# A two-block transformer layer on one core: eight modulation tiles contracted on PE, and the normed input's product on DVE

## The chip, the core and the metric

The kernel runs on one core of one Trainium2 chip. The metric is the device time of one execution in microseconds. The engines are PE (matmuls), DVE, ACT, POOL and SP; SP, ACT and POOL also issue DMAs.

## What is computed

Two blocks follow each other on x (1 x 256 tokens x 1024 features). The part that matters here is the beginning of the first:

```
mod = silu(c) @ w_ada + b_ada                    # c: 1 x 1024, w_ada: 1024 x 6144
shift1, scale1, gate1, shift2, scale2, gate2 = split(mod, 6)
h = rms_norm(x, norm1_w) * (1.0 + scale1) + shift1
proj = h @ w_in                                  # q, k, v, conv, index queries, keys and weights
...
x = x + gate1 * (y_mix @ w_out)                  # attention over 64 selected keys, and a short convolution
h2 = rms_norm(x, norm2_w) * (1.0 + scale2) + shift2
x = x + gate2 * peer_ffn(h2, ...)                # 16 of 16384 experts for each of 8 heads and token
x = second_block(x, ...)                         # 2 layers: window attention, gated spatial mixing
```

All of it is in float32.

## The kernel before

The kernel is written engine by engine: each has its own program with waits on semaphores, and nothing is reordered. The order within an engine is the order of its lines.

The input is held transposed, as 8 chunks of 128 features by 256 tokens (`xT`, `hT`). A projection's weights come in units of up to 1 MB (8 chunks by 256 columns) into a ring of four (`wring`, L256). Each 128 columns of a unit are a piece. To reach float32 accuracy with the fast matmul, a piece is split in two rounded parts: ACT makes the high part (`whi`, `split_hi`, L544) and DVE or POOL the low part (`wlo`, `split_lo`, L551); `LO_1` says who. The input is split in the same way (`xh` on ACT at L839, `xl` on DVE in `h_low`, L1575). PE multiplies three of the four combinations (L1155 to L1157). Units 0 and 1 hold the index queries (pieces 0 to 3), unit 2 the index keys and weights (piece 4 and 8 columns more).

The modulation is 48 tiles of 128 columns of w_ada. A tile is loaded transposed, 128 columns on the partitions by 1024 rows, 512 KB, into a ring of five (`ada`). DVE multiplies it by silu(c), which is broadcast over the partitions (`cbc`), and sums along the row (`ada_dots`, L1529). Tiles 0 to 15 give scale1 and shift1, two for each chunk of the input, and come first. SP loads them (`load_ada`, L663), each waiting for the dot that frees its slot, with unit 0 behind the twelfth (`UNIT_0_AFTER`) and units 1 to 3 behind the sixteenth. Later tiles follow certain units (`ADA_AFTER`).

The first stage is then:

- ACT: silu of `cbc`, the squares of x (L818), x times norm1_w into `hT` (L821), the square root (L824). Then for each chunk, once its scale and shift are there, two products with bias (L839), one rounded (`xh`) and one not (`hT`). Pieces 0 and 1 are rounded ahead of chunk 6, pieces 2 and 3 after chunk 7.
- PE: the sum of the squares (L1204), and then the projections (`whole`).
- DVE: for each chunk two dots, the gain (L1585) and the shift with its bias (L1587); the reciprocal of the root after chunk 2's dots (L1583); the lowered chunks as they come. Pieces 0 to 3 are lowered behind chunk 6 and at the end. Then tiles 16 to 23 (`ada_tiles`), whose bias add is L1534, and the index scores (L1604, L1607).
- POOL: `hT` times the reciprocal (L753), then its own pieces from piece 4 on. Piece 12 and later stand behind the mask of the index scores (L759).

SP's queue stands in order too. Unit 6 waits until PE is done with unit 2, since it takes its slot; tiles 21 to 24 are behind units 6 and 7.

After the projections come attention, the experts' stage (two thirds of the span, its pairs of rows gathered by POOL's DMAs) and the second block. None of these is touched.

Of the kernel before, what the change touches and what calls it, by code (L numbers as in the profile page):

```python
# [14 lines left out]
ALU = mybir.AluOpType  # L15
ACT = mybir.ActivationFunctionType
# [6 lines left out]
P = 128  # L23
T = 256
NT = T // P
D = 1024
KC = D // P
# [13 lines left out]
PRING = 4  # L41
WUNIT = KC * 256
WPIECE = KC * P
ADA_RING = 5
UNIT_0_AFTER = 12
ADA_TILES = 6 * D // P
SLOTS, LOW_SLOTS = 14, 8
PAIRS = SLOTS - LOW_SLOTS
# [1 line left out]
EXPERTS = 4  # L50


N1W, N2W, B_ADA, CONV_W, CONV_B, ATT_W, CNV_W, Q_W, K_W, COLS = 0, 8, 16, 64, 76, 80, 84, 88, 89, 90

BQ, BK, BV, BUG, BZG, BZA, LCOLS = 0, 4, 5, 6, 10, 14, 18

# [61 lines left out]

ADA_AFTER = {3: range(16, 21), 6: (21, 22), 7: (23, 24), 8: (25, 26), 9: (27, 28), 18: range(29, 40), }
PIECES_1, SPAN_1 = pieces(UNITS_1[:MIX_UNITS])
LO_1 = "d" * 4 + "p" * 17 + "d" * 16
assert len(LO_1) == len(PIECES_1)
def ada_column(n):

    return n if n >= 2 * KC else n // 2 + (KC if n % 2 == 0 else 0)


def starts(units):  # L130
# [115 lines left out]
def build(nc, a, out):  # L246
    ctx = ExitStack()
    with ctx:
        def sb(name, shape, dt=F32):
            return ctx.enter_context(nc.sbuf_tensor(name, shape, dt))  # L250

        def sem(name):
            return ctx.enter_context(nc.semaphore(name))
# [8 lines left out]
        xT = sb("xT", [P, KC, T])  # L262
        hT = sb("hT", [P, KC, T])
# [58 lines left out]
        u = w1.take(HC * (T + 2)).rearrange("p (c t) -> p c t", t=T + 2)  # L322
        cb = w1.take(HC * T).rearrange("p (c t) -> p c t", t=T)
        yaT = iqT
        relu = p_buf

        w2 = Area(work[:, :])
# [74 lines left out]
        w_loaded = [sem(f"w_loaded{s}") for s in range(RING)]  # L402
        ada_loaded = [sem(f"ada_loaded{s}") for s in range(ADA_RING)]
        ada_used = sem("ada_used")
        last_ada_loaded, last_ada_used = sem("last_ada_loaded"), sem("last_ada_used")
        pool_chain, dve_chain, act_chain = sem("pool_chain"), sem("dve_chain"), sem("act_chain")
        const_ready = sem("const_ready")
        c_silu = sem("c_silu")
        squares = sem("squares")
        sums = sem("sums")  # L410
        h_weighted, rstd_ready, mod_ready = sem("h_weighted"), sem("rstd_ready"), sem("mod_ready")
        std_ready = sem("std_ready")
        h_ready = sem("h_ready")
        h_scaled = sem("h_scaled")
# [242 lines left out]
        def _(sp):  # L657
            sp.dma_start(xT[:, :, :], a["xT"].rearrange("c p t -> p c t")).then_inc(x_loaded, 16)

            def load_ada(n):  # L660
                if n >= ADA_RING:
                    sp.wait_ge(ada_used, n - ADA_RING + 1)
                sp.dma_start(ada[:, n % ADA_RING, :], a["w_ada"][ada_column(n)]).then_inc(ada_loaded[n % ADA_RING], 16)  # L663

            def load_unit(n):
                sp.dma_start(wring[:, n % RING, 0:AT_1[n + 1] - AT_1[n]], a["w1"][:, AT_1[n]:AT_1[n + 1]]).then_inc(w_loaded[n % RING], 16)

            for n in range(2 * KC):
                load_ada(n)
                if n == UNIT_0_AFTER - 1:  # L670
                    load_unit(0)
            for n, (name, at, width, chunks) in enumerate(UNITS_1):
                if n >= RING:
                    was = n - RING
                    if was < MIX_UNITS:
                        split_wait(sp, last_piece(was, PIECES_1))
                        if UNITS_1[was][0] == "idx":
                            sp.wait_ge(proj, DONE_1[last_piece(was, PIECES_1)] + 1)
                    elif UNITS_1[was][0] == "wq":
                        sp.wait_ge(queries, UNITS_1[was][1] // P + 2)  # L680
                    else:
                        sp.wait_ge(expert_scores, UNITS_1[was][1] // (2 * KEYS) + 2)
                if n:
                    load_unit(n)
                for k in ADA_AFTER.get(n, ()):
                    load_ada(k)
                if n == MIX_UNITS + 2:
                    sp.wait_ge(proj, M1)
                    sp.dma_start(last_ada, a["w_ada"][LAST_ADA:].rearrange("n p d -> p n d")).then_inc(last_ada_loaded, 16)
# [42 lines left out]
        def _(pool):  # L732
# [14 lines left out]
            pool.iota(count16[:, :], pattern=[[1, PICKS]], base=0, channel_multiplier=0).then_inc(const_ready, 1)  # L747
            pool.memset(u[:, :, 0:2], 0.0).then_inc(const_ready, 1)

            pool.wait_ge(rstd_ready, 1)  # L750
            for c in range(KC):
                pool.wait_ge(h_weighted, c + 1)
                pool.tensor_tensor(hT[:, c, :], hT[:, c, :], rstd[:, :], ALU.mult).then_inc(h_scaled, 1)  # L753
            for n in range(4, 12):
                split_lo(pool, "p", n)

# [51 lines left out]
        def _(act):  # L808
# [2 lines left out]
            act.dma_start(cols[:, :], a["cols"]).then_inc(cols_loaded, 16)  # L811
            act.wait_ge(c_loaded, 16)
            nc.scalar.activation(cbc, cbc, ACT.Silu).then_inc(c_silu, 1)


            act.wait_ge(x_loaded, 16)
            for c in range(KC):
                nc.scalar.activation(sq[:, c, :], xT[:, c, :], ACT.Square).then_inc(squares, 1)  # L818
            act.wait_ge(cols_loaded, 16)
            for c in range(KC):  # L820
                nc.scalar.activation(hT[:, c, :], xT[:, c, :], ACT.Copy, scale=cols[:, N1W + c:N1W + c + 1]).then_inc(h_weighted, 1)  # L821
            act.wait_ge(const_ready, 2)
            act.wait_ge(sums, 1)
            nc.scalar.activation(rstd[:, :], aux[:, 0, 0:T], ACT.Sqrt, bias=eps[:, 0:1], scale=1.0 / D).then_inc(std_ready, 1)  # L824
            rounded = [0]
# [1 line left out]
            def round_to(n):  # L827

                for k in range(rounded[0], n):
                    split_hi(act, k)  # L830
                rounded[0] = n

            for c in range(KC):
                if 2 * c == UNIT_0_AFTER:
                    round_to(2)
                act.wait_ge(h_scaled, c + 1)
                act.wait_ge(mod_ready, 2 * c + 2)
                for h in (xh, hT):
                    ins = nc.scalar.activation(h[:, c, :], hT[:, c, :], ACT.Identity, bias=mod[:, c:c + 1], scale=gain[:, c:c + 1])  # L839
                ins.then_inc(h_ready, 1)  # L840
            round_to(PRING)

            act.dma_start(wsT[:, :, :], a["wsT"].rearrange("g s t -> s g t")).then_inc(par_loaded, 16)
            act.dma_start(sink[:, :, :].rearrange("p l h -> p (l h)"),
# [294 lines left out]
        def _(pe):  # L1139
# [19 lines left out]
            def input_parts(ready, count):  # L1159

                seen = set()

                def chunk_parts(k):
                    if k not in seen:
                        pe.wait_ge(ready, count(k))
                        seen.add(k)
                    return xh[:, k, :], xl[:, k, :]
                return chunk_parts
# [33 lines left out]
            for c in range(KC):  # L1202
                pe.wait_ge(squares, c + 1)
                ins = mm(aux[:, 0, 0:T], ones[:, :], sq[:, c, :], start=(c == 0), stop=(c == KC - 1))  # L1204
            ins.then_inc(sums, 1)
            h_in = input_parts(h_split, lambda k: k + 1)
            whole(h_in, 3)

# [311 lines left out]
        def _(dve):  # L1520
# [2 lines left out]

            def ada_dots(lo, hi):

                for n in range(lo, hi):
                    dve.wait_ge(ada_loaded[n % ADA_RING], 16 * (n // ADA_RING + 1))
                    tile = ada[:, n % ADA_RING, :]
                    v.tensor_tensor_reduce(tile, tile, cbc, 1.0, 0.0, ALU.mult, ALU.add,  # L1529
                                           mod[:, ada_column(n):ada_column(n) + 1]).then_inc(ada_used, 1)  # L1530

            def ada_bias(lo, hi):
                dve.wait_ge(ada_used, hi)
                chain.link(v.tensor_tensor(mod[:, lo:hi], mod[:, lo:hi], cols[:, B_ADA + lo:B_ADA + hi], ALU.add))  # L1534

            def ada_tiles(lo, hi):
# [30 lines left out]
            def low_to(n):  # L1567

                for k in range(lowered[0], n):
                    split_lo(dve, "d", k)  # L1570
                lowered[0] = n

            def h_low(c):
                dve.wait_ge(h_ready, c + 1)
                v.tensor_tensor(xl[:, c, :], hT[:, c, :], full(xh[:, c, :]), ALU.subtract).then_inc(h_split, 1)  # L1575

            dve.wait_ge(const_ready, 3)

            for c in range(KC):
                ada_dots(2 * c, 2 * c + 2)  # L1580
                if c == 2:
                    dve.wait_ge(std_ready, 1)
                    v.reciprocal(rstd[:, :], rstd[:, :]).then_inc(rstd_ready, 1)  # L1583
                dve.wait_ge(ada_used, 2 * c + 2)
                v.tensor_scalar(gain[:, c:c + 1], mod[:, KC + c:KC + c + 1], cols[:, B_ADA + KC + c:B_ADA + KC + c + 1], ones[:, 0:1],  # L1585
                                ALU.add, ALU.add).then_inc(mod_ready, 1)
                v.tensor_tensor(mod[:, c:c + 1], mod[:, c:c + 1], cols[:, B_ADA + c:B_ADA + c + 1], ALU.add).then_inc(mod_ready, 1)  # L1587
                for k in {3: (0, 1), 4: (2, 3), 5: (4,), 6: (5,), 7: (6,)}.get(c, ()):
                    h_low(k)
                if 2 * c == UNIT_0_AFTER:  # L1590
                    low_to(1)
            h_low(KC - 1)
            low_to(4)
            ada_tiles(2 * KC, 3 * KC)


# [481 lines left out]
```

## Time and profile before

| | |
|---|---|
| median of 3 runs | 1270.02 us (1266.65 to 1270.06) |
| profiled execution | 1264.54 us |
| its span | 1262.8 us |
| granted TensorE clock, mean | 0.947 |
| PE busy | 1079.4 us (85%) |
| DVE busy | 832.7 us (66%) |
| ACT busy | 435.2 us (34%) |
| POOL busy | 404.7 us (32%) |
| moved by DMA | 390.36 MB, 309 GB/s |

The span is the time from the first to the last instruction in the trace; the execution's own time adds 1.7 us around it. Times in the trace are microseconds from the span's start. The clock is the share of 2.4 GHz that TensorE was granted.

### The profile page before, as it was taken

What the parts mean: (1) busy time and instruction counts of PE and PEld (TensorE: products, weight loads), DVE (VectorE), ACT (ScalarE), POOL (GpSimd) and SP (SyncE); (2) the same over time, 40 slices, a digit from 0 to 9 for tenths busy, and PEclk for the clock granted to TensorE, in tenths of its full rate; (3) what the DMA queues carried; (4) which work ended last, traced back from release to release, by engine and by line L of the source; (5) the groups of instructions that cost most, each with busy time, mean ns of one, the idle gap of its engine ahead of it and who ended that gap; (6) DMA issues with size and microseconds to landing.
All of it is one profiled execution on the core that took longest, in us unless ns stands there. A gap on an engine that the chain in (4) does not pass through costs nothing.

```text
span 1262.8 us, 19024 instructions
## 1 busy us (share of the span) xinstructions
PE 1079.4 (85%) x7676; PEld 1007.5 (80%) x7676; DVE 832.7 (66%) x1750; ACT 435.2 (34%) x907; POOL 404.7 (32%) x344
## 2 busy tenths in 40 slices
PE   1789998778998978787878788788999997999997
PEld 1789887778988878787777787688898786898785
DVE  6779878756676666676776677456644656634656
ACT  4543823122123212222122212213465443465542
POOL 3364003432343333333333333332200254400251
PEclk8899998899999998999898989989999899999999
DMA  8875457999999999999999999998545454344450
GB/s 332 315 280 176 151 197 281 422 421 420 420 421 420 421 419 421 420 421 421 420 421 421 420 422 420 422 420 330 188 167 201 137 201 162 134 167 167 146 187 34
DMA packets 60233, 390.36 MB, mean 309 GB/s; under 512 B 6769, under 2 KB 8817, under 8 KB 16370
## 3 DMA queue, kind: packets, MB, share of 16 engines
q0 software_dynamic: 36864, 268.45, 51.2%
q1 hardware_dynamic: 21666, 119.58, 26.1%
q8 instruction: 60, 0.98, 0.3%
q10 hardware_dynamic: 1616, 1.12, 0.3%
q14 instruction: 27, 0.22, 0.0%
HBM read 388.08 MB, written 1.05 MB: 308 GB/s over the span
## 4 chain that ended last, share of the span: by engine, by line
PE 48%; DMA 35%; DVE 8%; ACT 4%; POOL 3%; issue 2%; SPq 0%; DVEq 0%; POOLq 0%; ACTq 0%
DMA low_pairs<-in_peer_uv,work 20%; DMA rows<-in_peer_uv,work 14%; PE aux L1343 11%; PE pj L1419 5%; PE pj L1420 5%; PE pj L1421 5%; PE pj L1155 5%; PE pj L1157 4%; PE pj L1156 4%; PE aux L1322 3%; DVE rows L1529 2%; DMA rows<-in_w_ada 1%; ACT rows L900 1%; DVE low_pairs L1785 1%; PE aux L1272 1%
## 5 line engine op out<-in xcount | busy, mean ns | idle before, releaser
L1343 PE MATMUL aux<-work,low_pairs 128*128 128x128 f32 x2304 | 283.3, 287 | 57.8 <-ACT work L1012 57.8
L1343 PEld LDWEIGHTS aux<-work,low_pairs 128*128 128x128 f32 x2304 | 276.4, 202 | 64.4 <-ACT work L1012 64.4
L1343 PE MATMUL aux<-work,rows 128*128 128x128 f32 x1792 | 227.1, 292 | 54.8 <-ACT work L1012 54.8
L1343 PEld LDWEIGHTS aux<-work,rows 128*128 128x128 f32 x1792 | 221.5, 207 | 60.0 <-ACT work L1012 60.0
L783 POOL DMA_INDIRECT low_pairs<-in_peer_uv,work x144 | 135.2, 939 | 217.9 <-PE aux L1343 215.4
L783 POOL DMA_INDIRECT rows<-in_peer_uv,work x112 | 108.8, 971 | 257.0 <-PE aux L1343 178.6
L1155 PE MATMUL pj<-xh,whi 128*128 128x256 f32 x552 | 160.2, 290 | 34.1 <-DVE wlo L551 23.0
L606 POOL TENSOR_TENSOR wlo<-wring,whi 128x1024 fp32r<-128x1024 f32 x34 | 85.4, 2523 | 273.8 <-ACT whi L599 273.8
L606 DVE TENSOR_TENSOR wlo<-wring,whi 128x1024 fp32r<-128x1024 f32 x74 | 103.6, 1423 | 83.3 <-ACT whi L599 82.8
L1156 PE MATMUL pj<-xl,whi 128*128 128x256 f32 x552 | 157.7, 286 | 0.0
L1157 PE MATMUL pj<-xh,wlo 128*128 128x256 f32 x552 | 157.7, 286 | 0.0
L1007 ACT ACTIVATE work<-work 128x4 f32<-128x4 f32 (+1 forms) x66 | 13.7, 208 | 382.0 <-DVE work L1785 382.0
L1155 PEld LDWEIGHTS pj<-xh,whi 128*128 128x128 f32 x552 | 107.3, 194 | 37.6 <-DVE wlo L551 23.6
L1785 DVE CUSTOM_DVE_ANT_0 low_pairs<-low_pairs,aux 128x1024 f32<-128x1024 f32 x72 | 87.0, 1220 | 57.5 <-DMA low_pairs<-in_peer_uv,work 57.3
L599 ACT CAST whi<-wring 128x1024 fp32r<-128x1024 f32 x108 | 110.5, 1051 | 32.3 <-PE pj L1421 32.1
L1156 PEld LDWEIGHTS pj<-xl,whi 128*128 128x128 f32 x552 | 107.4, 195 | 0.2 <-issue 0.2
L1785 DVE CUSTOM_DVE_ANT_0 low_pairs<-low_pairs,pj 128x1024 f32<-128x1024 f32 x72 | 85.9, 1218 | 32.8 <-DMA low_pairs<-in_peer_uv,work 32.6
L1157 PEld LDWEIGHTS pj<-xh,wlo 128*128 128x128 f32 x552 | 107.2, 194 | 0.0
L1785 DVE CUSTOM_DVE_ANT_0 rows<-rows,aux 128x1024 f32<-128x1024 f32 x56 | 67.7, 1219 | 43.4 <-DMA rows<-in_peer_uv,work 43.3
L1419 PE MATMUL pj<-whi,xh 128*128 128x512 f32 x224 | 91.9, 410 | 5.1 <-POOL wlo L606 2.2
L1420 PE MATMUL pj<-whi,xl 128*128 128x512 f32 x224 | 89.4, 399 | 0.0
L1421 PE MATMUL pj<-wlo,xh 128*128 128x512 f32 x224 | 89.3, 399 | 0.0
(242 smaller groups left out, 1546.7 us busy)
## 6 DMA issues: line engine op xcount, KB each, us to landing
wring<-in_w SPq DMA_DIRECT2D x80, 1024.0 KB, 4.9
rows<-in_w_ada SPq DMA_DIRECT2D x40, 512.0 KB, 6.1
low_pairs<-in_w_ada SPq DMA_DIRECT2D x1, 4096.0 KB, 13.3
low_pairs<-in_peer_uv,work POOLq DMA_INDIRECT x144, 23.4
work<-in_late_rows SPq DMA_DIRECT2D x2, 1024.0 KB, 9.5
xT<-in_norm_rows SPq DMA_DIRECT2D x2, 1024.0 KB, 7.5
rows<-in_gate_rows SPq DMA_DIRECT2D x2, 1024.0 KB, 6.8
rows<-in_peer_uv,work POOLq DMA_INDIRECT x112, 22.8
```

Of the source, the lines that this page charges most:

```text
L599: nc.scalar.copy(layer_part(whi, l, p), layer_raw(l, p)).then_inc(w_hi, 1)
L606: eng.tensor_tensor(layer_part(wlo, l, p), layer_raw(l, p), full(layer_part(whi, l, p)), ALU.subtract).then_inc(w_lo[who], 1)
L783: pool.indirect_dma_start(out=pair(n), out_offset=None, in_=a["peer_uv"], in_offset=bass.IndirectOffsetOnAxis(ap=expert[g % EXPERTS][:, j: ...
L1155: mm(o, w[0], x[0], start=start, stop=False)
L1156: mm(o, w[0], x[1], start=False, stop=False)
L1157: return mm(o, w[1], x[0], start=False, stop=stop)
L1322: ins = mm(aux[:, 4 + s, ts], w[:, k, s * P:(s + 1) * P], hT[:, k, ts], start=(k == 0), stop=(k == KC - 1))
L1343: ins = mm(peer_sum[t][:, c * P:(c + 1) * P], pair(n)[:, D + c * P:D + (c + 1) * P], diag[:, n % PICKS, :], start=(n % (EXPERT_HEADS * PIC ...
L1419: mm(bank(u), hi[:, k, ts], w_hi_[:, j, :], start=(k == 0), stop=False)
L1420: mm(bank(u), lo[:, k, ts], w_hi_[:, j, :], start=False, stop=False)
L1421: ins = mm(bank(u), hi[:, k, ts], w_lo_[:, j, :], start=False, stop=(k == last))
L1785: v.tensor_tensor_reduce(row, row, h2_tok[g // EXPERT_HEADS], 1.0, 0.0, ALU.mult, ALU.add, dots[g % 2][:, j:j + 1]).then_inc(dotted, 1)
```

## The change

Eight of the first sixteen tiles, those of the input's chunks 1, 3, 4 and 5, are loaded untransposed (`w_ada_pe`: 128 rows on the partitions, 8 blocks of 128 columns). Each has a place of its own, six in room that is used later and two in `qn` and `kn`. PE contracts each in 8 products with a column of silu(c) (`c_col`), into banks 1 to 4 of `aux`. DVE makes the gain and the shift of these chunks out of PSUM (`pe_mod`); those of the other four, whose dots stay on DVE, go to POOL. The product of x, norm1_w and the reciprocal is one operation on DVE. A table load for the square root is asked for ahead of the squares. SP loads the tiles in the order of the chunks, with unit 0 behind chunk 1's. ACT rounds pieces 0 and 1 ahead of chunk 0 and pieces 2 and 3 ahead of chunk 1. DVE lowers pieces 0 and 1 among the products and pieces 2 and 3 behind chunk 0. Tiles 16 to 39 are loaded as before, with new numbers.

```diff
-UNIT_0_AFTER = 12
+UNIT_0_AFTER = 2
...
-ADA_AFTER = {3: range(16, 21), 6: (21, 22), 7: (23, 24), 8: (25, 26), 9: (27, 28), 18: range(29, 40), }
+ADA_AFTER = {3: range(8, 13), 6: (13, 14), 7: (15, 16), 8: (17, 18), 9: (19, 20), 18: range(21, 32), }
+PE_CHUNKS, DVE_CHUNKS = (1, 3, 4, 5), (0, 2, 6, 7)
+PE_TILES = 2 * len(PE_CHUNKS)
...
+def pe_ada_column(n):
+    return PE_CHUNKS[n // 2] + (KC if n % 2 == 0 else 0)
...
+        mix_rows = flat[:, ADA_RING * D:ADA_RING * D + 6 * D].rearrange("p (s d) -> p s d", d=D)
+        pe_ada = [mix_rows[:, n, :] for n in range(6)] + [qn.rearrange("p c t -> p (c t)"), kn.rearrange("p c t -> p (c t)")]
...
 # SP
-            for n in range(2 * KC):
-                load_ada(n)
-                if n == UNIT_0_AFTER - 1:
+            for c in range(KC):
+                if c == UNIT_0_AFTER:
                     load_unit(0)
+                for s in range(2):
+                    if c in PE_CHUNKS:
+                        n = 2 * PE_CHUNKS.index(c) + s
+                        sp.dma_start(pe_ada[n], a["w_ada_pe"][n]).then_inc(pe_ada_loaded[n], 16)
+                    else:
+                        load_ada(2 * DVE_CHUNKS.index(c) + s)
...
 # POOL
-            pool.wait_ge(rstd_ready, 1)
-            for c in range(KC):
-                pool.wait_ge(h_weighted, c + 1)
-                pool.tensor_tensor(hT[:, c, :], hT[:, c, :], rstd[:, :], ALU.mult).then_inc(h_scaled, 1)
+            pool.wait_ge(cols_loaded, 16)
+            for i, c in enumerate(DVE_CHUNKS):
+                pool.wait_ge(ada_used, 2 * i + 2)
+                pool.tensor_scalar(gain[:, c:c + 1], mod[:, KC + c:KC + c + 1], cols[:, B_ADA + KC + c:B_ADA + KC + c + 1], 1.0,
+                                   ALU.add, ALU.add).then_inc(mod_ready_pool, 1)
+                pool.tensor_tensor(mod[:, c:c + 1], mod[:, c:c + 1], cols[:, B_ADA + c:B_ADA + c + 1], ALU.add).then_inc(mod_ready_pool, 1)
...
 # ACT
+            act.wait_ge(cols_loaded, 16)
+            nc.scalar.activation(c_col[:, :], cols[:, C_COL:C_COL + KC], ACT.Silu).then_inc(c_silu, 1)
+            act.wait_ge(const_ready, 2)
+            nc.scalar.activation(warm[:, :], eps[:, 0:1], ACT.Sqrt)
...
-            for c in range(KC):
-                nc.scalar.activation(hT[:, c, :], xT[:, c, :], ACT.Copy, scale=cols[:, N1W + c:N1W + c + 1]).then_inc(h_weighted, 1)
...
+            round_to(2)
             for c in range(KC):
-                if 2 * c == UNIT_0_AFTER:
-                    round_to(2)
+                if c == 1:
+                    round_to(PRING)
                 act.wait_ge(h_scaled, c + 1)
-                act.wait_ge(mod_ready, 2 * c + 2)
+                if c in PE_CHUNKS:
+                    act.wait_ge(mod_ready_dve, 2 * PE_CHUNKS.index(c) + 2)
+                else:
+                    act.wait_ge(mod_ready_pool, 2 * DVE_CHUNKS.index(c) + 2)
...
-            round_to(PRING)
...
 # PE, between the sum of squares and the projections
+            pe.wait_ge(c_silu, 2)
+            for n in range(PE_TILES):
+                pe.wait_ge(pe_ada_loaded[n], 16)
+                for k in range(KC):
+                    ins = mm(aux[:, 1 + n // 2, n % 2:n % 2 + 1], pe_ada[n][:, k * P:(k + 1) * P], c_col[:, k:k + 1], start=(k == 0), stop=(k == KC - 1))
+                if n % 2:
+                    ins.then_inc(pe_ada_done, 1)
...
 # DVE
+            def pe_mod(c):
+                i = PE_CHUNKS.index(c)
+                dve.wait_ge(pe_ada_done, i + 1)
+                v.tensor_scalar(gain[:, c:c + 1], aux[:, 1 + i, 0:1], cols[:, B_ADA + KC + c:B_ADA + KC + c + 1], ones[:, 0:1],
+                                ALU.add, ALU.add).then_inc(mod_ready_dve, 1)
+                v.tensor_scalar(mod[:, c:c + 1], aux[:, 1 + i, 1:2], cols[:, B_ADA + c:B_ADA + c + 1], None, ALU.add).then_inc(mod_ready_dve, 1)
+
+            ada_dots(PE_TILES, PE_TILES + 2)
+            dve.wait_ge(std_ready, 1)
+            chain.link(v.reciprocal(rstd[:, :], rstd[:, :]))
+            dve.wait_ge(x_loaded, 16)
             for c in range(KC):
...
+                v.scalar_tensor_tensor(hT[:, c, :], xT[:, c, :], cols[:, N1W + c:N1W + c + 1], rstd[:, :], ALU.mult, ALU.mult).then_inc(h_scaled, 1)
+                if c == 1:
+                    low_to(2)
+            ada_dots(PE_TILES + 2, PE_TILES + 4)
+            pe_mod(1)
+            h_low(0)
+            low_to(4)
+            h_low(1)
+            pe_mod(3)
+            h_low(2)
+            pe_mod(4)
+            h_low(3)
+            pe_mod(5)
+            ada_dots(PE_TILES + 4, PE_TILES + 6)
+            h_low(4)
+            h_low(5)
+            ada_dots(PE_TILES + 6, PE_TILES + 8)
+            h_low(6)
             h_low(KC - 1)
-            low_to(4)
             ada_tiles(2 * KC, 3 * KC)
```

Where the instructions stand now. First ACT, from the root to the first chunks: before, with the casts of pieces 0 and 1 ahead of chunk 6 and those of pieces 2 and 3, which wait for unit 1 (`w_loaded1`), at the end:

```order
L824 ACTIVATE rstd<-aux,eps 128x256 [waits const_ready]
L839 ACTIVATE xh<-hT,mod,gain 128x256 [waits mod_ready,h_scaled]
L839 ACTIVATE hT<-hT,mod,gain 128x256
...
L839 ACTIVATE xh<-hT,mod,gain 128x256 [waits mod_ready,h_scaled]
L839 ACTIVATE hT<-hT,mod,gain 128x256
L544 CAST whi<-wring 128x1024 [waits w_loaded1]
L544 CAST whi<-wring 128x1024
```

and in the change (its lines are numbered anew; L860 is L839, L555 is L544):

```order
L841 ACTIVATE rstd<-aux,eps 128x256 [waits sums]
L555 CAST whi<-wring 128x1024 [waits w_loaded0]
L555 CAST whi<-wring 128x1024
L860 ACTIVATE xh<-hT,mod,gain 128x256 [waits mod_ready_pool,h_scaled]
L860 ACTIVATE hT<-hT,mod,gain 128x256
L555 CAST whi<-wring 128x1024 [waits w_loaded1]
L555 CAST whi<-wring 128x1024
L860 ACTIVATE xh<-hT,mod,gain 128x256 [waits mod_ready_dve,h_scaled]
L860 ACTIVATE hT<-hT,mod,gain 128x256
```

The wait for unit 1 has moved from behind chunk 7 to ahead of chunk 1.

Then SP, from its first DMA to unit 3, in the change (`wring` rows are units 0 to 3, `in_w_ada_pe` are PE's tiles):

```order
L669 DMA xT<-in_xT 128x8x256
L674 DMA rows<-in_w_ada 128x1024 x2
L685 DMA rows<-in_w_ada_pe 128x1024 x2
L677 DMA wring<-in_w 128x2048
L674 DMA rows<-in_w_ada 128x1024 x2
L685 DMA rows<-in_w_ada_pe 128x1024 x4
L685 DMA work<-in_w_ada_pe 128x1024 x2
L674 DMA rows<-in_w_ada 128x1024
L674 DMA rows<-in_w_ada 128x1024 [waits ada_used] x3
L677 DMA wring<-in_w 128x2048
L677 DMA wring<-in_w 128x1088
L677 DMA wring<-in_w 128x2048
```

Unit 0 is the fifth transfer behind x instead of the thirteenth; units 1 to 3 stay behind all sixteen tiles, of which three instead of eleven wait for a dot.

Last DVE, from the dots of chunk 2 to the end of the first stage, in the change (L1556 are the dots, L1602 the lowered chunks, L562 the lowered pieces, L1610 and L1612 the gain and shift of a PE chunk):

```order
L1556 ISA rows,mod<-rows 128x1024 [waits ada_loaded3]
L1556 ISA mod 128x1
L1610 TENSOR_SCALAR gain<-aux,cols,ones 128x1 [waits pe_ada_done]
L1612 TENSOR_SCALAR mod<-aux,cols 128x1
L1602 TENSOR_TENSOR xl<-hT,xh 128x256 [waits h_ready]
L562 TENSOR_TENSOR wlo<-wring,whi 128x1024 [waits w_hi] x2
L1602 TENSOR_TENSOR xl<-hT,xh 128x256 [waits h_ready]
L1610 TENSOR_SCALAR gain<-aux,cols,ones 128x1 [waits pe_ada_done]
L1612 TENSOR_SCALAR mod<-aux,cols 128x1
...
L1556 ISA rows,mod<-rows 128x1024 [waits ada_loaded4]
L1556 ISA mod 128x1
```

The lowering of pieces 2 and 3 stands between the lowered chunks 0 and 1, ahead of the dots of chunks 6 and 7.

## Rows read from the trace of the kernel before

**Rows 1.** Chain of waits, first 43 us: start, duration, engine, what it wrote, line.
```profile
1.29 8.68 DMA rows<-in_w_ada
...
17.84 1.68 DVE rstd L1583
...
38.35 1.14 DVE rows L1529
...
39.53 0.27 DVE gain L1585
...
39.97 0.48 ACT xh L839
40.48 0.60 ACT hT L839
41.09 0.42 DVE xl L1575
41.52 1.15 DVE wlo L551
42.71 0.39 PE pj L1155
```

**Rows 2.** Chain of waits, later.
```profile
57.89 0.13 PE pj L1157
...
60.29 10.03 DMA rows<-in_w_ada
...
83.88 2.34 POOL wlo L551
...
91.36 0.36 PE pj L1155
...
156.41 1.67 DVE low_pairs L1691 x4
```

**Rows 3.** Windows: us, busy PE, PEld, DVE, ACT, POOL (count), clock, DMA share, GB/s.
```profile
0.00:5.00 5.00, 0.00 (x0) 0.00 (x0) 0.00 (x0) 1.28 (x1) 1.75 (x15) 1.00 0.50 148
5.00:10.00 5.00, 0.70 (x2) 0.65 (x3) 0.00 (x0) 2.32 (x6) 0.00 (x0) 1.00 1.05 382
10.00:15.00 5.00, 4.80 (x16) 3.59 (x14) 4.83 (x9) 4.60 (x14) 0.00 (x0) 1.00 1.03 410
15.00:20.00 5.00, 0.00 (x0) 0.00 (x0) 4.96 (x12) 1.65 (x2) 0.40 (x1) 0.98 1.03 409
20.00:25.00 5.00, 0.00 (x0) 0.00 (x0) 4.16 (x9) 3.01 (x6) 5.00 (x5) 0.50 0.96 365
...
35.00:40.00 5.00, 2.74 (x13) 2.74 (x14) 4.93 (x13) 1.93 (x4) 0.00 (x0) 0.50 0.99 401
...
40.00:41.00 1.00, 1.00 (x9) 1.00 (x9) 0.21 (x1) 1.00 (x3) 0.00 (x0) 0.86 0.99 401
```

**Rows 4.** Timeline: start, duration (of a group: first to last), engine, line, operation.
```profile
0.82 0.10 POOL L735 MEMSET eps<- 128x1 f32 x1
...
9.30 5.51 PE L1204 MATMUL aux<-low_pairs,ones 128*128 128x256 f32 x16 [9.30 <-ACT low_pairs L818]
...
19.60 10.19 POOL L753 TENSOR_TENSOR hT<-hT,rstd 128x256 f32<-128x256 f32 x8 [16.93 <-DVE rstd L1583]
...
40.97 1.03 ACT L544 CAST whi<-wring 128x1024 fp32r<-128x1024 f32 x1
...
48.81 0.54 PEld L1218 LDWEIGHTS pj<-wring,hT 128*128 128x128 f32 x4
...
49.27 0.19 PEld L1155 LDWEIGHTS pj<-xh,whi 128*128 128x128 f32 x1
...
1073.20 1.12 PE L1442 MATMUL aux<-ident,work 128*128 128x128 f32 x4 [2.88 <-DVE work L1898]
1073.97 0.78 PE L1419 MATMUL pj<-whi,xh 128*128 128x512 f32 x1
```

**Rows 5.** The loads at L1204 in the stretch 11.3 to 12.3.
```profile
L1204 PEld LDWEIGHTS aux<-low_pairs,ones x3: 333/333/333, 11.1 to 12.0; 128*128 128x128 f32 x3
```

More of the change, by code:

```diff
@@ L50 @@
 EXPERTS = 4
-N1W, N2W, B_ADA, CONV_W, CONV_B, ATT_W, CNV_W, Q_W, K_W, COLS = 0, 8, 16, 64, 76, 80, 84, 88, 89, 90
+N1W, N2W, B_ADA, CONV_W, CONV_B, ATT_W, CNV_W, Q_W, K_W, C_COL, COLS = 0, 8, 16, 64, 76, 80, 84, 88, 89, 90, 98
 BQ, BK, BV, BUG, BZG, BZA, LCOLS = 0, 4, 5, 6, 10, 14, 18
@@ L125, in ada_column @@
 def ada_column(n):
-    return n if n >= 2 * KC else n // 2 + (KC if n % 2 == 0 else 0)
+    return n + PE_TILES if n >= 2 * len(DVE_CHUNKS) else DVE_CHUNKS[n // 2] + (KC if n % 2 == 0 else 0)
+def pe_ada_column(n):
+    return PE_CHUNKS[n // 2] + (KC if n % 2 == 0 else 0)
 def starts(units):
@@ L284, in build @@
         bn = sb("bn", [P, NT, 6])
+        c_col = sb("c_col", [P, KC])
         mv = sb("mv", [P, NT, 2])
@@ L404, in build @@
         ada_used = sem("ada_used")
+        pe_ada_loaded, pe_ada_done = [sem(f"pe_ada_loaded{n}") for n in range(PE_TILES)], sem("pe_ada_done")
         last_ada_loaded, last_ada_used = sem("last_ada_loaded"), sem("last_ada_used")
@@ L410, in build @@
         sums = sem("sums")
-        h_weighted, rstd_ready, mod_ready = sem("h_weighted"), sem("rstd_ready"), sem("mod_ready")
+        mod_ready_dve, mod_ready_pool = sem("mod_ready_dve"), sem("mod_ready_pool")
         std_ready = sem("std_ready")
@@ L818, in _ @@
                 nc.scalar.activation(sq[:, c, :], xT[:, c, :], ACT.Square).then_inc(squares, 1)
-            act.wait_ge(cols_loaded, 16)
-            for c in range(KC):
-                nc.scalar.activation(hT[:, c, :], xT[:, c, :], ACT.Copy, scale=cols[:, N1W + c:N1W + c + 1]).then_inc(h_weighted, 1)
-            act.wait_ge(const_ready, 2)
             act.wait_ge(sums, 1)
@@ L1524, in ada_dots @@
             def ada_dots(lo, hi):
-                for n in range(lo, hi):
+                for n in range(lo - PE_TILES, hi - PE_TILES):
                     dve.wait_ge(ada_loaded[n % ADA_RING], 16 * (n // ADA_RING + 1))
@@ L1532, in ada_bias @@
             def ada_bias(lo, hi):
-                dve.wait_ge(ada_used, hi)
+                dve.wait_ge(ada_used, hi - PE_TILES)
                 chain.link(v.tensor_tensor(mod[:, lo:hi], mod[:, lo:hi], cols[:, B_ADA + lo:B_ADA + hi], ALU.add))
@@ L1577, in _ @@
             dve.wait_ge(const_ready, 3)
-            for c in range(KC):
[L1580 to L1591, printed above, removed]
+            def pe_mod(c):
[8 more added lines that the diff above has]
+            dve.wait_ge(x_loaded, 16)
+            for c in range(KC):
+                v.scalar_tensor_tensor(hT[:, c, :], xT[:, c, :], cols[:, N1W + c:N1W + c + 1], rstd[:, :], ALU.mult, ALU.mult).then_inc(h_scaled, 1)
[16 more added lines that the diff above has]
+            h_low(6)
             h_low(KC - 1)
-            low_to(4)
             ada_tiles(2 * KC, 3 * KC)
@@ L2048 @@
         "w_ada": x["w_ada"].T.reshape(ADA_TILES, P, D),
+        "w_ada_pe": np.stack([x["w_ada"][:, pe_ada_column(n) * P:(pe_ada_column(n) + 1) * P].reshape(KC, P, P).transpose(1, 0, 2).reshape(P, D)
+                              for n in range(PE_TILES)]),
         "w1": units(UNITS_1, part | {
@@ L2055 @@
                                 col(x["attn_out_norm_w"][order1]), col(x["conv_out_norm_w"]),
-                                col(np.concatenate([x["q_norm_w"]] * 2)), col(np.concatenate([x["k_norm_w"]] * 2))], 1),
+                                col(np.concatenate([x["q_norm_w"]] * 2)), col(np.concatenate([x["k_norm_w"]] * 2)), col(x["c"])], 1),
         "w2": np.stack([layer_units({n: cut(w2[l], n, z) for n, z in dict(kv=2 * P, vg=512, ug=512, zg=512, za=512, ga=D, gg=D).items()} | {
```

## The prediction

> **What bounds the kernel now.** I read the chain of waits first, in order of time, because the change touches only the first 48 us of a span of 1262.8 us and the question is whether that stretch sets the end. It does. The chain [rows 1] runs without a gap from the first transfer to the projections: DVE's dots of the modulation tiles, the reciprocal, POOL's product, then turns of DVE and ACT until DVE lowers the last chunk of the input (41.09) and weight piece 1 (41.52), and PE streams from 42.71. From there PE is dense to 57.89. That end lets SP issue the next unit and the next modulation tiles, the last of which lands at 70.3, so that DVE can go on to the index scores, behind which POOL's next lowering stands (83.88), which PE waits for (91.36) [rows 2]. So what delays PE's stream at 42.7 delays the tiles, the scores and all that follows, one for one; nothing in those rows starts by another clock. The number to work out is when PE can start piece 1, against 42.71.
>
> Then the traffic. Over the first 20 us the windows give 148, 382, 410 and 409 GB/s [rows 3], which is 0.74 + 1.91 + 2.05 + 2.05 = 6.75 MB by 20.0. After 20 the rate falls to 365 because SP waits for slots of the ring of five. The transfers are then held by DVE, not by the queue. The granted clock is 0.50 (1.2 GHz) from 20 on, after PE's last work ended at 14.8. PE starts again at 37.26 (2.74 us busy in the stretch 35 to 40, all at 0.50) and the clock returns between 40 and 41 [rows 3, 4].
>
> **The sixteen tiles, now unheld.** Eight of them have places of their own and need no free slot; SP's waits (the dots of tiles 0 to 2) end before the queue runs dry. I take 0.41 MB/us throughout. Bytes ahead of a landing: x 1.05, c 0.52, cols 0.05, unit 0 1.05, each tile 0.524. The two tiles of chunk 5 are the eleventh and twelfth: 1.62 + 6.29 + 1.05 = 8.96 MB, moved by 20 + 2.21/0.41 = 25.4. All sixteen and unit 1: 12.11 MB, by 20 + 5.36/0.41 = 33.1. The first tile's bytes (2.14 MB) are moved by 8.7 and it lands at 10.0 (1.29 + 8.68) [rows 1], so I add 1.4, rounded up by 0.1: **tile 12 at 26.8, tile 16 at 31.9, unit 1 at 34.5**.
>
> **The wait that the change adds.** ACT now rounds pieces 2 and 3, which lie in unit 1, ahead of chunk 1's scale and shift. Unit 1 is queued behind all sixteen tiles. Before, ACT did this after the last chunk. PE's sum ended at 14.8 and now ends about 1 later; ACT has the root by about 16.5, rounds pieces 0 and 1 (2 x 1.03) and gives chunk 0 (1.1), so it is done by 20; from there it stands until 34.5, and behind it in its queue stand the products of chunks 1 to 7. DVE stands too: its lowering of chunk 1 is queued behind pieces 2 and 3, and behind that the dots of chunks 6 and 7. PE waits for the lowered chunks. That is the step on which the forecast rests.
>
> From 34.5 on, with durations of [rows 1, 4]: two casts at 1.03 leave ACT free at 36.5. A pair of products takes 0.48 + 0.60 = 1.08, a new pair every 1.0; DVE's lowering of a chunk 0.41; the gain and bias of a chunk 0.44 (from the gain at 39.53 to ACT's start at 39.97). Chunk 1 leaves ACT at 37.6, DVE lowers it by 38.3 (pieces 2 and 3, 1.15 each, end at 37.9), gain 3 by 38.7, chunk 2 lowered by 39.1, gain 4 by 39.5, chunk 3 by 40.1, gain 5 by 40.6. Dots of chunk 6, 2 x 1.14 [rows 1]: 42.9; chunks 4 and 5 lowered by 43.6; dots of chunk 7 to 45.9. POOL's two small operations are not in the trace: between its 128x1 memsets (0.10) and its 128x256 product (10.19/8 = 1.27), I take 0.2 each, near the first since they have one column [rows 4]. ACT's pair for chunk 7: 46.3 to 47.4, lowered by 47.8. Before that was 41.5. PE's three matmuls of the chunk at the slow clock, 0.64: piece 1 starts at 48.4 against 42.71, **+5.7**.
>
> **What goes and gives nothing.** ACT's eight weighted copies and POOL's eight products (10.19) go; in their place are eight fused products on DVE, 1.67/4 = 0.42 each, 3.4 in all, and the lowering of pieces 0 and 1 (2.3) [rows 2, 4]. One table load moves from behind the sum to before the squares, where it and the column's silu put PE's sum off by about 1. DVE has the root at 16.5, and the reciprocal (1.7 [rows 1]), the products, the two pieces and the dots of chunk 2 (2.3) end by 26, under the wait for unit 1: price 0. If unit 1 were early, this chain would set the time together with tile 16. DVE's eight dots fewer (9.1) lie under the same wait.
>
> **PE's dots.** 64 products, each two instructions (the 8-column matmuls at L1218: four for two products). The loads of four of them run from 48.81 to 49.27, 0.115 each at full clock [rows 4]: a tile of 16 takes 1.8, all 14.7. At the slow clock the bounds are 0.19 (four transposes, 1073.20 to 1073.97) and 0.33 (a whole load, not overlapped) [rows 4, 5]; I take 0.21, nearer to the first, since loads run under matmuls in it, so 3.4 a tile. The clock fell 5 us after PE's last wide work; a 1-column product is the nearest thing to none in the trace, so I let it fall at about 20. Tiles 3 to 8 from 20.4 then end at 40.9, and gain 5 comes at 41.4 instead of 40.6: **+0.8**. With full clock they end at 31.0, which costs 0. If the clock never rises before, all eight end at 17.1 + 27.3 = 44.4, and gain 5 comes 4.3 later: +4.3. Below nothing is excluded, since unit 1 holds the rest.
> The Trainium skill ("TensorE: Matmul & The Clock Gate", LDWEIGHTS) puts a load at columns/1.2 ns, 107 ns, at either clock. By it the dots would end at about 31 and this term be 0.
>
> **The clock after.** Before, the slow stretch lay under waits. Now PE's work between 41 and 48 is in bits with gaps, so I take the clock as slow at 48.4. The rise took 3 to 4 us of PE's work from 37.26 [rows 3]; I take 3.4. Half of it is lost: **+1.7** (0, if the bits before count, to 3.4, if the rise takes twice as long).
>
> The Trainium skill ("DMA: Bandwidth & Descriptors", Anatomy of one DMA) gives 2.0 us plus bytes at 436 GB/s. By that, an estimate, unit 1 would land at 30.6 and the sum be 3.9 less. This trace's stretches without a hold show 409 and 410, which decide.
>
> **Sum.** 5.7 + 0.8 + 1.7 = +8.2 us on the profiled execution's 1264.54, that is 1272.7. That execution is 5.5 under the median of the runs, 1270.02, so as a median **1278.2 us**. About 0.3% (3.8 us) is what a measurement of this kernel tells from no change.
>
> **Rivals.**
> *PE's dots become the bound.* If each load stands alone, 128 x 0.33 = 42 us after 16, ending at 58.5; gain 5 and from it the same 7.2 to the last chunk (40.6 to 47.8) give 66.1, 18.3 later than 47.8. With the +5.7 and +1.7 that is +25.7, 1295.7. For it: nothing so narrow stands back to back in the trace. Against: all loads seen overlap. 6%.
> *The delay is absorbed.* A transfer or DVE's selection downstream has slack that the chain hides, and PE's late stream is made up by 90 us: no change, 1270, within 1267 to 1274. For it: DVE waits for a transfer of 10.03 there [rows 2]. Against: those transfers are issued only when PE is done. 17%.
> *The other side: the start is bound by tile 16.* If unit 1 landed before ACT wants it, or ACT's wait ended early, the last chunk would be lowered at 31.9 + 1.1 + 0.4 + 1.1 + 0.4 = 34.9, 6.6 before 41.5, so 1263.4. It decides from the landing of unit 1: with +8.2 at 34.5, the change breaks even at 26.3. For it: the tiles no longer wait for slots and DVE loses eight dots, which is real work off the chain of [rows 1]. Against: landing at 26.3 means 5.36 MB in the 4.9 us after 20, 1.09 MB/us. Only another service order in the queue could do it. 12%.
>
> **How the numbers follow.** Forecast 65% (1274 to 1284: landing of unit 1 by 2 us either way, clock 0 to 3.4, dots up to +4.3), absorbed 17%, faster start 12%, dots 6%. The range 1268 to 1285 leaves out the last two. Faster by over 0.3% (under 1266.2): 0.12. Within: 0.18 (the absorbed case and a little of the forecast's edge). Slower: 0.70.
>
> **What would show it.** In the new profile: ACT's third cast (L555) with a wait of some 14 us on unit 1 ending at 34 to 35; chunk 7's lowering (L1602) at 47 to 48; PE's dots (L1230) at 0.11 or 0.21 each, ended before 42; PE's piece 1 at 48 to 49; idle PE between 42 and 48. The landing of tiles 21 to 24 at 78 instead of 70. Wrong if the third cast starts before 28, if the dots run past 45, or if PE's start at 91.36 is not later by the same 7 to 9 us.

## The result and the profile after

The changed kernel takes 1279.22 us (median of 7 runs, 1273.78 to 1281.23) against 1270.06 for the kernel before (7 runs, 1266.65 to 1271.59): +9.2 us, a ratio of 1.0072 with a 95% interval of 1.0054 to 1.0091. It is slower. The forecast was 1278.2. Its profiled execution took 1278.93 with a span of 1277.2 and a mean clock of 0.939; that is 14.4 more than the span before. The two executions also differ in how the clock fell in the second block: 48 matmuls of it begin 9.4 later (969.68 against 960.24), the same matmuls of its second layer 12.8 later (1162.88 against 1150.06), and between 970 and 1020 the clock is 0.90 here and was 0.93 in the same work before. So I follow the shift from place to place, not by the spans.

The chain of waits of the changed kernel, its first 50 us (start, duration, what). It answers to [rows 1]:

```profile
10.30 5.73 PE aux L1224 x16
...
16.56 1.76 DVE rstd L1616
18.35 0.88 DVE hT L1619 x2
19.23 2.27 DVE wlo L562 x2
21.50 2.38 DVE hT L1619 x6
23.88 1.14 DVE rows L1556
25.05 0.33 SPq L674
25.42 9.59 DMA wring<-in_w
35.03 1.05 ACT whi L555
36.11 2.36 DVE wlo L562 x2
...
40.34 0.43 DVE xl L1602
40.77 0.19 DVE gain L1610
40.96 0.13 DVE mod L1612
41.09 1.13 DVE rows L1556
42.22 1.14 DVE rows L1556
43.37 0.67 DVE xl L1602 x2
44.04 1.14 DVE rows L1556
45.18 1.14 DVE rows L1556
46.43 0.53 POOL gain L769
46.96 0.16 POOL mod L771
47.20 0.45 ACT xh L860
...
48.33 0.44 DVE xl L1602
48.81 0.58 PE pj L1175
```

The transfer of unit 1 stands in it with 9.6 us. ACT's third cast begins at 35.03, when it has landed. Chunk 7 is lowered at 48.77, where before it was at 41.51. The timeline of ACT says how long it stood:

```profile
19.38 0.59 ACT L860 ACTIVATE hT<-hT,mod,gain 128x256 f32<-128x256 f32 x1
35.03 1.99 ACT L555 CAST whi<-wring 128x1024 fp32r<-128x1024 f32 x2 [15.07 <-DMA wring<-in_w]
36.93 0.60 ACT L860 ACTIVATE xh<-hT,mod,gain 128x256 fp32r<-128x256 f32 x1
```

PE in the timeline, with its narrow products in three groups (two tiles, four tiles, two tiles) and its first projection matmul behind them:

```profile
15.85 3.63 PE L1230 MATMUL aux<-c_col,rows 128*128 128x1 f32 x32
20.39 13.07 PE L1230 MATMUL aux<-c_col,rows 128*128 128x1 f32 x64 [0.91 <-DMA rows<-in_w_ada_pe]
33.32 6.96 PE L1230 MATMUL aux<-c_col,work 128*128 128x1 f32 x32
40.15 0.56 PE L1175 MATMUL pj<-xh,whi 128*128 128x256 f32 x1
```

Each product is two matmul instructions, and the rows and windows count these. The first 32 take 0.11 each (3.63/32), the last 96 take 0.21 (20.39 to 40.15). The windows show the clock under them; the columns are those of [rows 3], the clock is the third figure from the end:

```profile
15.00:20.00 5.00, 4.48 (x37) 4.29 (x35) 3.40 (x4) 3.56 (x5) 0.00 (x0) 1.00 1.02 409
20.00:25.00 5.00, 4.61 (x25) 4.61 (x26) 5.00 (x11) 0.00 (x0) 0.00 (x0) 0.62 1.03 412
25.00:30.00 5.00, 5.00 (x25) 5.00 (x25) 1.82 (x7) 0.00 (x0) 0.59 (x2) 0.50 1.02 406
30.00:35.00 5.00, 5.00 (x25) 5.00 (x25) 0.00 (x0) 0.00 (x0) 0.00 (x0) 0.50 1.03 422
...
45.00:50.00 5.00, 2.61 (x10) 2.02 (x10) 3.44 (x9) 2.19 (x4) 0.91 (x3) 0.50 0.77 258
50.00:55.00 5.00, 5.00 (x37) 5.00 (x36) 4.48 (x8) 1.29 (x3) 0.00 (x0) 0.80 0.99 401
```

PE is busy for all of 25 to 35 and the granted clock is 0.50. DMA runs at 406 to 422 GB/s without a hole, and DVE does nothing from 30 to 35.

Later in the chain (answers to [rows 2]; the first line begins when SP has issued the last of tiles 21 to 24):

```profile
68.13 10.12 DMA rows<-in_w_ada
...
91.82 2.35 POOL wlo L562
94.21 0.58 PE pj L1175
...
166.31 1.67 DVE low_pairs L1735 x4
```

Against before the transfer begins 7.8 later (60.29), POOL's lowering 7.9 (83.88), and the second norm's product 9.9 (156.41). The shift goes through everything.

### The profile page after: what moved, and what is told of

Read it like the earlier page. It is cut to its first block, busy times and chain, and to the rows that moved or that the text cites. A ratio compares the mean times of both kernels' runs of the same rounds, so it can differ in the third digit from the quotient of the medians.

```text
span 1277.2 us, 19259 instructions
## 1 busy us (share of the span) xinstructions
PE 1109.3 (87%) x7804; PEld 1036.8 (81%) x7804; DVE 819.9 (64%) x1734; ACT 432.6 (34%) x901; POOL 397.8 (31%) x344
## 4 chain that ended last, share of the span: by engine, by line
PE 52%; DMA 32%; DVE 7%; ACT 5%; issue 2%; POOL 1%; SPq 0%; ACTq 0%; DVEq 0%; POOLq 0%
DMA low_pairs<-in_peer_uv,work 21%; PE aux L1370 13%; DMA rows<-in_peer_uv,work 9%; PE pj L1446 5%; PE pj L1447 5%; PE pj L1448 5%; PE pj L1175 5%; PE pj L1177 4%; PE pj L1176 4%; PE aux L1349 4%; DVE low_pairs L1829 1%; ACT rows L920 1%; PE aux L1299 1%; PE aux L1278 1%; POOL wlo L617 1%
## 5 line engine op out<-in xcount | busy, mean ns | idle before, releaser
L1370 PE MATMUL aux<-work,rows 128*128 128x128 f32 x1792 | 219.9, 286 | 48.0 <-ACT work L1032 46.1
L1370 PEld LDWEIGHTS aux<-work,rows 128*128 128x128 f32 x1792 | 214.5, 201 | 53.1 <-ACT work L1032 50.8
L1175 PE MATMUL pj<-xh,whi 128*128 128x256 f32 x552 | 163.5, 296 | 14.1 <-DVE xl L1740 4.0
L1176 PE MATMUL pj<-xl,whi 128*128 128x256 f32 x552 | 160.5, 291 | 0.0
L1177 PE MATMUL pj<-xh,wlo 128*128 128x256 f32 x552 | 160.5, 291 | 0.0
L1175 PEld LDWEIGHTS pj<-xh,whi 128*128 128x128 f32 x552 | 110.3, 200 | 17.7 <-issue 9.5
L1176 PEld LDWEIGHTS pj<-xl,whi 128*128 128x128 f32 x552 | 110.5, 200 | 0.2 <-issue 0.2
L1177 PEld LDWEIGHTS pj<-xh,wlo 128*128 128x128 f32 x552 | 110.3, 200 | 0.0
```

The lines of the kernel that those rows point to most:

```text
L1175: mm(o, w[0], x[0], start=start, stop=False)
L1176: mm(o, w[0], x[1], start=False, stop=False)
L1177: return mm(o, w[1], x[0], start=False, stop=stop)
L1370: ins = mm(peer_sum[t][:, c * P:(c + 1) * P], pair(n)[:, D + c * P:D + (c + 1) * P], diag[:, n % PICKS, :], start=(n % (EXPERT_HEADS * PIC ...
```

## The experiments

Two things stand late at once in the changed kernel: ACT's casts, by unit 1, and gain 5, which DVE wants at 40.68 and which PE's products allow from 40.2. The first four runs take them apart. Beside each time stands the start of the transfer of the last of tiles 21 to 24 in the run's chain, which is 60.29 in the kernel before. The kernel before took 1270.54 beside the first four (21 runs) and 1270.50 beside the last four (26 runs). The expectations give the start of chunk 7's lowering (48.3 in the changed kernel), the measurements its end (48.8), 0.4 later.

**Casts late.** The changed kernel with:

```diff
-                if c == 1:
-                    round_to(PRING)
...
+            round_to(PRING)          # ACT, behind chunk 7
...
             h_low(0)
-            low_to(4)
...
             h_low(KC - 1)
+            low_to(4)
```

> The changed kernel, with ACT's casts of pieces 2 and 3 behind chunk 7 again and DVE's lowering of them at the end, as before the change. In the changed kernel chunk 7 is lowered at 48.3 and PE's narrow products end at 40.2. Theory A (two bounds stand equally late: unit 1's landing, which gives gain 5 at 40.7, and the products at the slow clock, which allow it from 40.2): the last chunk is lowered at 47.5 to 48.5, the time stays 8 to 10 us above the kernel before. Rival B (the wait for unit 1 alone is the cause): the last chunk is lowered by 41 or earlier, the time is within 2 us of the kernel before.

Measured: 1279.2 us, ratio 1.0065 (1.0042 to 1.0088), transfer at 69.22. As if nothing had been undone. ACT no longer waits for unit 1, but for the gains of PE's chunks, in its timeline:

```profile
27.34 0.60 ACT L858 ACTIVATE xh<-hT,mod,gain 128x256 fp32r<-128x256 f32 x1 [6.62 <-DVE mod L1611]
...
34.89 0.60 ACT L858 ACTIVATE xh<-hT,mod,gain 128x256 fp32r<-128x256 f32 x1 [4.50 <-DVE mod L1611]
41.72 0.60 ACT L858 ACTIVATE xh<-hT,mod,gain 128x256 fp32r<-128x256 f32 x1 [5.74 <-DVE mod L1611]
```

Chunk 5 leaves for ACT at 41.72 (41.20 in the changed kernel), and chunk 7 is lowered at 49.3. Theory A holds (the lowering starts at 48.87, 0.4 outside its interval), rival B falls.

**Wide products.** The changed kernel with the moving column repeated:

```diff
-  mm(aux[:, 1 + n // 2, n % 2:n % 2 + 1], pe_ada[n][:, k * P:(k + 1) * P], c_col[:, k:k + 1], ...)
+  mm(aux[:, 1 + n // 2, n % 2 * P:n % 2 * P + P], pe_ada[n][:, k * P:(k + 1) * P], c_col[:, k:k + 1].broadcast_to([P, P]), ...)
...
-  v.tensor_scalar(mod[:, c:c + 1], aux[:, 1 + i, 1:2], ...)
+  v.tensor_scalar(mod[:, c:c + 1], aux[:, 1 + i, P:P + 1], ...)
```

> The changed kernel, with the moving column of PE's products repeated over 128 columns (same result, 128 times), everything else unchanged, the wait for unit 1 too. Theory A (the clock falls because the products are one column wide): the granted clock stays 1.00 through the products, each takes 0.12 and not 0.21, they end at 31 to 33 instead of 40.2; chunk 7 is lowered no earlier than 47.5, since the wait for unit 1 remains, and the time stays 8 to 10 us above the kernel before. Rival B (width is not what holds the clock): the clock is 0.50 from 22 on and the products take 0.21 or more each. Rival C (the products alone are the cause): the time falls by 5 us or more.

Measured: 1277.18 us, ratio 1.0059 (1.0038 to 1.0080), transfer at 69.32. The windows:

```profile
20.00:25.00 5.00, 4.26 (x38) 4.26 (x39) 5.00 (x11) 0.00 (x0) 0.00 (x0) 1.00 1.03 409
25.00:30.00 5.00, 5.00 (x47) 5.00 (x46) 1.58 (x5) 0.00 (x0) 0.59 (x2) 1.00 1.03 408
30.00:35.00 5.00, 2.08 (x19) 1.88 (x17) 0.00 (x0) 0.00 (x0) 0.00 (x0) 0.94 1.03 424
```

47 matmul instructions in 5 us instead of 25, at the full clock, and the last begins at 31.5. A product 128 times as wide takes half the time, as the clock is twice as high. Where both versions run at the full clock, on the first two tiles, they take the same within 0.1 us (3.63 with one column):

```profile
15.61 3.73 PE L1230 MATMUL aux<-c_col,rows 128*128 128x128 f32 x32
```

But ACT still starts its casts at 35.02 and chunk 7 is lowered at 48.8. The time is 2.0 under the changed kernel, inside the noise of these runs. Theory A holds in the clock, the products and chunk 7. Its time came out lower, 6.6 above the kernel before instead of 8 to 10, with an interval (4.8 to 10.2) that reaches into the forecast one. Rivals B and C fall.

**Both.** The two edits together.

> Both edits together: casts of pieces 2 and 3 late, and the products 128 columns wide. Theory A (both bounds must go): products end at 31 to 33, chunk 5 is lowered by 36, dots of chunk 7 end at 37 to 38 (DVE's order still puts the four last dots behind gain 5), chunk 7 lowered at 39.5 to 41, 8 us earlier than in the changed kernel; the time is -1 to +3 us against the kernel before. Rival: if either alone explains the loss, this run differs by less than 2 us from the better of the other two.

Measured: 1269.08 us, ratio 0.9989 (0.9978 to 1.0000), transfer at 60.44. The chain:

```profile
32.22 0.28 DVE gain L1609
...
37.97 0.53 POOL gain L769
38.50 0.16 POOL mod L771
...
39.86 0.44 DVE xl L1601
```

Products end by 32.2, chunk 7 is lowered at 40.3, and the whole loss is gone (the time is 1.5 under the kernel before, half a microsecond better than forecast). Neither edit alone moved the end clear of the noise; together they give back 10 us. That settles the cause: two waits that end within 0.6 us of each other (40.2 and 40.77 for gain 5). Gain 5 still waits 1.5 us for PE's products here.

**Dots early.** The last kernel with the order of DVE's last dots changed:

```diff
             h_low(3)
-            pe_mod(5)
             ada_dots(PE_TILES + 4, PE_TILES + 6)
+            pe_mod(5)
             h_low(4)
-            h_low(5)
             ada_dots(PE_TILES + 6, PE_TILES + 8)
+            h_low(5)
             h_low(6)
```

> The same as the last, and DVE does the dots of chunk 6 ahead of gain 5 and those of chunk 7 ahead of chunk 5's lowering, as the tiles land (tile 16 at about 32). Theory: chunk 7 lowered at 36 to 38; against the kernel before 4 us earlier, less what the clock costs (0 to 3.4): -5 to 0 us. If tile 16 lands later than 34, no gain over the last run.

Measured: 1268.41 us, ratio 0.9984 (0.9975 to 0.9994), transfer at 58.26, chunk 7 lowered at 38.7 (from 38.30, 0.3 outside the interval). It is the first version with an interval clear of the kernel before, by 0.16%; against the last kernel the difference is inside the noise of the times.

**Narrow again.** The same order, one column wide.

> As the last run of the first series (casts late, dots of chunks 6 and 7 moved ahead), but the products one column wide again. It tells whether the width matters once both other waits are gone. Theory A (the slow clock under narrow products then sets the time): products end at 40 to 41 at 0.21 each, gain 5 at 41.2, chunk 7 lowered at 46 to 47, 8 us later than with wide products (38.3); the time is 5 to 9 us above the kernel before. Rival: with the dots early the products have slack, chunk 7 lowered by 40, time within 2 us of the kernel before.

Measured: 1274.75 us, ratio 1.0030 (1.0016 to 1.0044), transfer at 64.11. Products end at 40.5, chunk 7 is lowered at 46.3, 7.5 later than with wide products. The rival falls. The time is only 6.3 us over the wide version and 4.2 over the kernel before, under the 5 to 9 that I gave (its interval is 2.0 to 5.6). The timeline of PE shows what was gained:

```profile
43.65 0.41 PE L1176 MATMUL pj<-xh,wlo 128*128 128x256 f32 x1
44.12 0.54 PE L1174 MATMUL pj<-xh,whi 128*128 128x256 f32 x1
44.49 0.28 PE L1175 MATMUL pj<-xl,whi 128*128 128x256 f32 x1
```

Piece 0's matmuls run from 40.5 to 45.2 here with no gap over 0.1 us, and the clock is up by 44.5, before chunk 7, so that it costs nothing afterwards: the clock is 1.00 from 45 on.

**The fused product alone.** The kernel before, with only the second half of the change:

```diff
 # DVE, behind chunk 2's dots
-                    v.reciprocal(rstd[:, :], rstd[:, :]).then_inc(rstd_ready, 1)
+                    chain.link(v.reciprocal(rstd[:, :], rstd[:, :]))
+                    dve.wait_ge(x_loaded, 16)
+                    for k in range(KC):
+                        v.scalar_tensor_tensor(hT[:, k, :], xT[:, k, :], cols[:, N1W + k:N1W + k + 1], rstd[:, :], ALU.mult, ALU.mult).then_inc(h_scaled, 1)
 # ACT's weighted copies and POOL's products are gone
```

> The kernel before with only the second half of the change: x times norm1_w times the reciprocal in one operation on DVE, behind the reciprocal, in place of ACT's weighting and POOL's product. Theory A (a wash): 3.3 us more on DVE's chain, and back come the 0.5 us that each of five dots is longer while POOL multiplies (1.74 against 1.22) and the waits for POOL's first products: piece 1 within 1.5 us of 42.71, the time -1.5 to +1.5 us against the kernel before. Rival B (DVE's chain only grows): +3 us or more. Rival C (this is where the change earns): -2 us or more.

Measured: 1269.65 us, ratio 1.0002 (0.9991 to 1.0013), transfer at 60.03. Its timeline of DVE:

```profile
19.82 3.26 DVE L1579 SCALAR_TENSOR_TENSOR hT<-xT,cols,rstd 128x256 f32<-128x256 f32 x8
```

3.3 us more on DVE's chain, and PE starts piece 1 at 42.63 instead of 42.71. A wash, theory A. So the loss is in the other half.

**The clock held.** The kernel with late casts, wide products and early dots, and matmuls that nobody reads in PE's gaps:

```diff
-            whole(h_in, 3)
+            def keep_busy(k):
+                for _ in range({4: 5, 6: 3}.get(k, 0)):
+                    mm(aux[:, 5, 0:T], ones[:, :], sq[:, k, :], start=True, stop=True)
+            whole(h_in, 1, between=keep_busy)
+            whole(h_in, 2)
```

> The kernel with late casts, wide products and early dots (its clock fell to 0.50 at about 38 and rose at 43), and eight 128x256 matmuls more whose results nobody reads: five behind chunk 4's and three behind chunk 6's part of piece 0, to fill PE's gaps between 34 and 38. Theory: the clock stays at 1.00, what follows is earlier by half of the slow stretch, 1.5 to 3 us, less up to 1 us that the fillers hold up PE: the time 1 to 3 us under that of the kernel without them, 3 to 5 us under the kernel before. Rival (the slow stretch lies under waits): no difference, -1 to -3 us against the kernel before.

Measured: 1265.94 us, ratio 0.9968 (0.9958 to 0.9977), transfer at 55.80. The windows of the kernel without the fillers:

```profile
35.00:40.00 5.00, 2.87 (x11) 2.58 (x12) 3.05 (x8) 3.56 (x6) 0.80 (x2) 0.59 1.01 410
40.00:45.00 5.00, 5.00 (x33) 5.00 (x33) 5.00 (x9) 1.11 (x4) 0.00 (x0) 0.73 1.04 400
```

and with them:

```profile
35.00:40.00 5.00, 5.00 (x33) 4.25 (x32) 3.05 (x7) 3.08 (x5) 0.80 (x2) 1.00 1.01 409
40.00:45.00 5.00, 5.00 (x45) 5.00 (x43) 4.81 (x8) 2.00 (x4) 1.66 (x1) 1.00 1.05 399
```

45 instead of 33 matmuls begin between 40 and 45. The time is 2.5 under the kernel without the fillers by the medians and 2.0 by the two ratios, and 4.6 under the kernel before; the theory holds. The transfer starts 2.5 earlier. Of this, 0.6 is that this execution's reciprocal began earlier (16.79 against 17.42). The other 1.8 fits half of the slow stretch of the kernel without fillers, from chunk 7's first matmul at 38.78 to 42.75, which is 2.0.

**And the last gains on DVE.** The same, with gain and shift of chunks 6 and 7 on DVE:

```diff
+            dve_mod(6)     # gain and shift on DVE, behind chunk 6's dots
             pe_mod(5)
             h_low(4)
             ada_dots(PE_TILES + 6, PE_TILES + 8)
+            dve_mod(7)
```

> The last kernel, with gain and shift of chunks 6 and 7 on DVE instead of POOL. In the changed kernel POOL takes 0.8 from the dot of chunk 7 to ACT's product (46.43 to 47.20) and 1.8 for chunk 6. Expected: chunk 7 lowered 0.4 to 1 us earlier (37.3 to 38), the time lower by as much, which is at the edge of what three rounds tell.

Measured: 1264.71 us, ratio 0.9954 (0.9938 to 0.9971). It is the fastest, but its interval and the last one's overlap, so the step from POOL to DVE is not shown by the times. In its profile chunk 7 is lowered at 38.9 and not earlier, as that execution's reciprocal began at 17.77 instead of 16.79. From the start of the reciprocal it is 21.1 us instead of 21.3, less than the 0.4 to 1 expected. What the step gains stays open.

## Why the prediction was right, and where not

- *What is late at PE's stream is late at the end.* Shown. In ten kernels the start of the tile transfer (of one execution) and the median time go together: 55.8 and 1265.9, 57.5 and 1264.7, 58.3 and 1268.4, 60.0 and 1269.7, 60.3 and 1270.5, 60.4 and 1269.1, 64.1 and 1274.8, 68.1 and 1279.2, 69.2 and 1279.2, 69.3 and 1277.2. The difference is 1207 to 1211 in all, so this bears out shifts of over 4 us, not the small ones. The absorbed case is out. The sign named at 91.36 came out at 100.94, 9.6 later and so above the 7 to 9; PE's wait ahead of it ends 7.9 later (94.21 against 86.27), and the rest is the clock (below).
- *Traffic and the landing of unit 1.* 34.5 forecast, 35.0 measured. The windows show 406 to 422 GB/s, against 410 taken from [rows 3]. The Trainium skill's formula ("DMA: Bandwidth & Descriptors", Anatomy of one DMA) had given 30.6, an estimate; the trace disagrees, at 406 to 422 and not 436. The page gives that formula for a DMA that GpSimd issues, and these are SP's.
- *The wait that the change adds.* In place and size (15.07 us). As a cause it was half the story. The prediction gave it 5.7 of 8.2 us and PE's products 0.8. With the products at full clock the wait alone still costs the loss (1277.2), and without the wait the slow products alone cost it too (1279.2). The sum was right because it took the later of two; "that is the step on which the forecast rests" was not, since undoing that step alone gains nothing. The prediction had both waits and put the products' end even 0.8 later. It did not say that either wait alone holds nearly all of the loss.
- *From 34.5 to the last chunk.* Forecast 47.8, measured 48.8. Unit 1 is 0.5 of it. In the rest POOL's two operations took 0.53 and 0.16, with 0.09 and 0.08 of hand-over, where I had 0.4 in all. Piece 1 began at 49.62, +6.9 against +5.7.
- *PE's products.* 0.115 and 0.21 were forecast, 0.113 and 0.206 measured; the fall of the clock near 20 too. They ended at 40.2, not 40.9, so gain 5 came when DVE reached it (40.77) and the term of +0.8 was 0. Of that 0.7, 0.3 is rounding in the forecast: six tiles of 16 at 0.21 from 20.4 end at 40.6. The start of 17.1 in its case of a clock that never rises stands in no row; the products began at 15.85. The Trainium skill ("TensorE: Matmul & The Clock Gate", LDWEIGHTS) gives 107 ns for such a load and names no clock, and the prediction read it as either clock. The pace measured is near it at the full clock only, 113 ns; at the slow one it is 206 ns.
- *The clock after.* Slow until about 51.9, so half of 2.3 us, +1.1 against +1.7. The three terms as measured: 6.9 + 0 + 1.1 = 8.0, and the transfer starts 7.8 later. That the sum was forecast as 8.2 is in part luck: the terms were off by +1.2, -0.8 and -0.6, which cancel.
- *What was not in the sum.* 9.9 - 7.8 = 2 us more by the second norm. In this execution the clock is down again after PE's wait of 3.5 before 94.21 (0.52 between 94 and 100). Before, after the same wait (3.4, to 86.27), it was 1.00 between 86 and 92. The shift stands at 9.9 already by 113.01 (103.11 before). It was one execution each, so I don't claim it for the median, where +9.2 leaves 1.4 over.
- *The rivals.* The products as a bound by whole loads (0.33): no. Start set by tile 16: in no run. Even in the wide version with late casts and early dots, DVE waits for no transfer between 24 and 42. There the chain runs from the reciprocal (17.42) through DVE's products, pieces 0 and 1, the dots and the turns with ACT, and chunk 7 comes to 38.7, not 34.9. The prediction had this chain set the time together with tile 16 once unit 1 is early; the chain alone does.

## What to carry to other kernels

When a change adds a wait, look for a second one that ends at the same time before you undo the first: here either fix alone gains nothing clear of the noise, and both together 10 us. In an engine's program, as it is written here, every wait is also a wait of all that stands behind it, so a load that is needed late (pieces 2 and 3) must not be waited for early. A matrix-vector product on PE may be widened by repeating the column: at 128 columns it cost 0.1 us on two tiles at the same clock here, and the clock stayed up.

## What the runs showed of the hardware

The granted clock fell to 0.50 while PE's own row showed it busy without a break, with products of one column (windows 25 to 35). With 128 columns and the same loads it stayed at 1.00 from 20 to 30. It was so in all three profiled kernels with one column and in all five with 128.

The pairs of a 128x128 float32 load and a matmul of one column came every 0.113 us at the full clock and every 0.206 at the slow one. A load by itself is shown with 0.19 and 0.33 us. So the loads were slower with the clock.

And eight matmuls without use, some 3.8 us of PE (2.32 and 1.46), made the kernel 2.0 to 2.5 us faster.
